# Prompt's pair sums, expert choice and softmax differences moved from the prompt's top-k stage into the latents' recurrence

## What is computed

```python
# for the prompt (phase 0), then for the latents (phase 1)
h = rmsnorm(x) * (1 + scale) + shift
q, k, v, xr, xg, ga, gr = split(h @ w_in)
xc = dwconv(xr)                              # width 4
r, ig = sigmoid(blockdiag(xc, w_a)), sigmoid(blockdiag(xc, w_i))    # two directions
a = exp(-8 * r * softplus(-lam)); b = sqrt(1 - a*a) * ig * xc
rnn = scan(a, b)                             # the recurrence, forward and backward
r_out = (rnn * gelu(xg)) @ w_rnn_o
...
x = x + g_a * ((sigmoid(ga) * a_out + sigmoid(gr) * r_out) @ w_out)
# PEER, per token and per head of 8:
s  = h @ w_q @ keys                          # 2 x 128 scores
st, it = top_k(s, 16)                        # for each of the two halves
cand = st[0][:, None] + st[1][None, :]       # the pair sums, 256
best, pos = top_k(cand, 16)
eidx = (it[0] * 128 + it[1])[pos]            # the experts: rows of u_tab and v_tab
g = softmax(best)
y = sum_k g_k * gelu(u_tab[eidx_k] . x) * v_tab[eidx_k]
```

## Time and profile before

| | |
|---|---|
| median of 3 runs | 2406.46 us |
| profiled execution | 2402.87 us, span 2401.0 us |
| DVE busy | 1880.0 us, 78% of the span |
| PE busy | 1722.7 us, 72% |
| chain that ended last | DVE 41%, PE 18%, DMA 17%, POOL 9%, issue 7% |
| prompt's top-k stage on DVE | 252.4 to 321.4 us |
| latents' recurrence on DVE | 321.7 to 494.4 us |

### The profile page before, as it was taken

The page is one execution under the profiler, slowest core; times in us unless marked ns, Lnnn a source line. Parts: engine busy times, 40 slices in busy tenths (PEclk is TensorE's granted clock), DMA queues, the critical chain, the costliest instruction groups (busy, mean ns, idle before and its releaser), DMA issues.

```text
span 2401.0 us, 21809 instructions
## 1 busy us (share of the span) xinstructions
PE 1722.7 (72%) x6720; PEld 1066.3 (44%) x6720; DVE 1880.0 (78%) x3982; ACT 501.9 (21%) x1271; POOL 1038.8 (43%) x1028
## 2 busy tenths in 40 slices
PE   5798879999888998961326666599999995000285
PEld 4788734544365466530113334466566664000131
DVE  3642779756895576899999998888787977999955
ACT  2632226510042001110015565700000000000010
POOL 0000001146433443435756775344344456777574
PEclk8899889999999999985557777899999998555599
DMA  9797824469745875867989999699999999999997
GB/s 343 256 308 261 261 88 140 140 234 370 280 142 200 299 270 198 306 211 288 409 332 346 410 392 345 197 359 411 413 409 412 411 411 411 409 410 410 354 409 302
DMA packets 290092, 753.71 MB, mean 314 GB/s; under 512 B 21801, under 2 KB 133177, under 8 KB 288441
## 3 DMA queue, kind: packets, MB, share of 16 engines
q0 software_dynamic: 147456, 536.94, 58.8%
q1 hardware_dynamic: 142520, 215.39, 25.4%
HBM read 740.93 MB, written 11.31 MB: 313 GB/s over the span
## 4 chain that ended last, share of the span: by engine, by line
DVE 41%; PE 18%; DMA 17%; POOL 9%; issue 7%; ACT 3%; PEld 2%; SPq 1%; DVEq 0%; POOLq 0%; PEldq 0%; ACTq 0%
DMA attn<-in_peer_u_dram,eidx 7%; PE bank L831 6%; DVE big L1602 5%; DVE attn L1602 4%; PE pair L831 4%; DMA ring_more<-in_peer_u_dram,eidx 4%; DVE work L1602 3%; PE bank L1015 3%; POOL work L2194 3%; POOL big L2194 2%; POOL attn L2194 2%; DMA ring_more<-in_peer_v_dram,eidx 2%; DVE ring_more L1602 2%; PE bank L1063 2%; ACT work L1135 2%
## 5 line engine op out<-in xcount | busy, mean ns | idle before, releaser
L1063 PE MATMUL bank<-big,work 128*128 128x512 f32 x176 | 107.0, 745 | 365.5 <-ACT work L1135 263.0
L831 PE MATMUL bank<-big 128*128 128x512 f32 (+1 forms) x1120 | 340.8, 464 | 33.1 <-DVEq L1470 19.8
L2194 POOL DMA_INDIRECT h_all<-in_peer_u_dram,eidx x109 | 122.1, 1120 | 529.0 <-DVEq L2063 322.0
L831 PE MATMUL pair<-big 128*128 128x128 f32 (+1 forms) x1216 | 333.5, 431 | 10.5 <-issue 9.0
L1108 PE MATMUL bank<-h_all,big 128*128 128x512 f32 x608 | 267.9, 597 | 5.3 <-DMA h_all<-in_peer_v_dram 5.3
L831 PEld LDWEIGHTS bank<-big 128*128 128x128 f32 x1120 | 184.0, 202 | 183.7 <-issue 177.4
L831 PEld LDWEIGHTS pair<-big 128*128 128x128 f32 x1216 | 185.8, 195 | 144.2 <-issue 142.0
L2194 POOL DMA_INDIRECT attn<-in_peer_u_dram,eidx x166 | 163.2, 983 | 165.7 <-DVE dots L1602 100.1
L1063 PEld LDWEIGHTS bank<-big,work 128*128 128x128 f32 x176 | 37.2, 229 | 421.9 <-issue 389.7
L1108 PEld LDWEIGHTS bank<-h_all,big 128*128 128x128 f32 x608 | 180.6, 297 | 88.4 <-DMA h_all<-in_peer_v_dram 6.0
L1602 DVE CUSTOM_DVE_ANT_0 attn<-attn,pair 128x1024 f32<-128x1024 f32 x166 | 199.5, 1218 | 22.5 <-DMA attn<-in_peer_u_dram,eidx 20.2
(11 more groups left out here) (319 smaller groups left out, 3100.4 us busy)
## 6 DMA issues: line engine op xcount, KB each, us to landing
big<-in_w_in_dram SPq DMA_DIRECT2D x44, 1024.0 KB, 9.4
h_all<-in_peer_v_dram SPq DMA_DIRECT2D x76, 512.0 KB, 6.8
big<-in_w_ada_dram SPq DMA_DIRECT2D x24, 1024.0 KB, 9.3
big<-in_peer_w_q_dram SPq DMA_DIRECT2D x16, 1024.0 KB, 8.2
gf_row<-in_peer_v_dram SPq DMA_DIRECT2D x26, 512.0 KB, 6.7
work<-in_peer_v_dram SPq DMA_DIRECT2D x26, 512.0 KB, 6.8
big<-in_w_rnn_o_dram SPq DMA_DIRECT2D x8, 1024.0 KB, 6.6
big<-in_w_attn_o_dram SPq DMA_DIRECT2D x8, 1024.0 KB, 7.4
```

The source lines that it names most:

```text
L831: last = nc.tensor.matmul(u[:, 0:n], w[:, k, col:col + P], src[:, k, 0:n], start=(k == 0), stop=(k == KD - 1))
L1063: last = nc.tensor.matmul(psum[i][:, :], diag[:, (n - 1) % DIAGS, :], ring[r][:, i * 512:(i + 1) * 512], start=(k == first_by_tensor[c]), ...
L2194: g.indirect_dma_start(dst, None, ins["peer_" + table][0], bass.IndirectOffsetOnAxis(ap=eidx[:, c, k:k + 1], axis=0)).then_inc(landed, 16)
```

## The change

`best_sums`, `route0` and `best_diffs` leave the prompt's top-k stage. `route0(h)` now runs `best_sums` itself, all eight heads come from `serve` (LEFT0 is 8), and the last one is followed by `best_diffs`. In the recurrence of phase 1 the middle `serve` is `serve(0)` in blocks 0 to 4 and `serve(3)` in blocks 5 to 7. `gelu_dots(0)` stays where it is.

```diff
-            HEADS_IN_LOOP = 3
-            LEFT0 = PH - HEADS_IN_LOOP
+            LEFT0 = PH
 
             def route0(h):
 
+                best_sums(0, h)
                 experts(0, h, h + 1)
                 ids(0, h, h + 1)
+                if h == PH - 1:
+                    best_diffs(0)
...
-                    serve(1)
+                    serve(1 if ph == 0 else 3 if j >= 5 else 0)
                     if j + 1 < LB:
                         gelu_out(j + 1)
...
                         topk(-1, hp, scores0[:, hp, :])
                         if hp + 1 in ada_after:
                             add_bias(ada_after[hp + 1])
-                        if hp % 2:
-                            best_sums(0, hp // 2)
-                            if hp // 2 < HEADS_IN_LOOP:
-                                route0(hp // 2)
-                        if hp == HP - 1:
-                            best_diffs(0)
                         continue
```

## The result

The changed kernel takes 2417.78 us, median of five runs (2417.55 to 2422.06), against 2406.46 us (2403.84 to 2408.01). The medians differ by 11.3 us, where 10.7 was predicted; the ratio over all runs is 1.0053 with a 95% interval of 1.004 to 1.0067, so the change makes the kernel slower by some 10 to 16 us. The work left the top-k stage as intended and PE's wait of 13.21 us disappeared; a later wait took its place.

The account below looks back on a forecast made before the run. PE and DVE run at almost the same pace; with the moved work DVE bounds the recurrence. 8.2 us later bank plus 2.5 us cold clock gives +10.7 us: 2413.6 us profiled, 2417.2 us median, range 2405 to 2423.

Parts of the forecast that it names:

- What leaves the top-k stage, and where DVE starts: Top-k stage to first `serve`: 36.5 us removed, state copy at 289.9, DVE's first route 16.1 us earlier.
- The work ahead of the bank: Recurrence: 29.5 us more DVE work before the bank for `xr` 7 is free, which comes 8.2 us later.
- PE's clock: At `xr` 7: PE restarts at 1.2 GHz after its new wait, costing 2.5 us (bounds 0 to 2.9).
- From `xr` 7 to `ro` 0: Recurrence's end: PE's 62.4 us stay; added rows lie beside them, DVE's slack shrinks to 7 us.
- rival C: Recurrence, merge and flush: more cold clock, late rows and flush cost 16.3 us in all, 2422.8 us; chance 0.10.
- Behind `ro` 0: Merge and later: all shifts as a whole; two rows left to the flush cost 0, or 2.3 us uncovered.
- Rival A: Recurrence: moved work fits in DVE's idle time, kernel 16.1 us faster, 2390.3 us; chance 0.10.
- Rival B: At `xr` 0's weights or the DMA-bound 541 to 602 us: shift absorbed, 2406.5 to 2411.3 us; chance 0.13.

Follow-up runs that it names:

- e10_after_again: The changed kernel once more, no edit, on the same chip as e9: 2420.96 us against 2408.41 for the kernel before, ratio 1.0055.
- e1: Changed kernel with the eight `best_sums` and `best_diffs` back in the top-k stage: 2402.42 us against 2407.88 for the kernel before, ratio 0.9978.
- e5: As e4, but the middle `serve` gives three rows in blocks 6 and 7 only: 2392.93 us against 2407.03 for the kernel before, ratio 0.994.
- e7: As e4, with the middle `serve` behind `gelu_out(j + 1)`: 2395.28 us against 2407.03 for the kernel before, ratio 0.9944.
- e9: Changed kernel with nine unread matmuls in PE's wait between `v` 0 and `xr` 7: 2415.60 us against 2408.41 for the kernel before, ratio 1.003.
- e2: Changed kernel with the middle `serve` behind `gelu_out(j + 1)` in every block: 2415.28 us against 2407.88 for the kernel before, ratio 1.0027.
- e8: Changed kernel with five rows in place of three in the middle of blocks 6 and 7: 2418.39 us against 2407.03 before, ratio 1.0041.
- e4: Changed kernel with three heads back in the top-k stage, five and `best_diffs` served in the recurrence: 2399.72 us against 2407.88 before, ratio 0.9966.
- e6: Changed kernel with seven unread matmuls in PE's wait between `v` 0 and `xr` 7: 2415.73 us against 2407.03 for the kernel before, ratio 1.0039.

## Why the prediction was right

- *What leaves the top-k stage, and where DVE starts.* The state copy was put at 289.9 and stands at 291.37, with 1.8 us of offset, which `xr` 0 has too. The first `serve` starts 17.7 us behind `xr` 0 (311.72 - 294.01); 17.4 were predicted.
- *The work ahead of the bank.* A delay of 8.2 us was worked out (451.7 less 443.57 is 8.1). `xr` 7 comes 8.9 us later, counted from `xr` 0, and 8.4 us later in e10_after_again. The difference is made of small things, among them 1.99 us of wait at `conv(1)` in place of 1.7, and handovers of 0.2 us at each of the three added heads. e1 to e5 and e7 moved this work in both directions and by single rows, and the bank followed each time to within 1.5 us of what was expected (of the middle, where a range was given).
- *PE's clock.* 2.5 us were taken; 16.35 against 13.97 us is 2.4, at a granted clock of 0.50 in the first 4.6 us. In e9, where the wait is filled, they are gone.
- *From `xr` 7 to `ro` 0.* Nothing else changed: 69.55 us to DVE's first output whenever PE didn't restart cold, in four kernels and in e9. DVE's slack shrank from 10.89 to 5.17 us; I had said 7. But 10.89 less the 4.6 us of the four added rows is 6.3, and the six rows behind the recurrence took 8.9 us in place of 7.75, since two of them waited 0.28 and 1.36 us for their gathers; that leaves 5.2, and is the start of rival C.
- *Behind `ro` 0.* In this execution the merge and the rotary steps took 2.2 us longer (`ro` 0 to the first scores of attention: 669.53 - 519.25 = 150.3 against 148.1 us). In e10, the same kernel, they took 0.5 us longer. Over all twelve profiled executions here they took 147.3 to 150.4 us, and e2, e7 and e8 lie above the kernel before while e4, e5 and e6 lie below it. So I take the 2.2 us for scatter and not for a price of the change. The chance given to C was for this. The two rows that fall to the flush were covered, as the sum had it: DVE's wait ahead of the second merge's first output shrank from 13.03 to 10.38 us. The remaining 4 us between the two profiled executions lie behind attention. The profiled execution is one of two of the five that took 4.3 us more than the median, and where they come from stays open.
- *Rival A* fails at the point where it was said to be decided: 29.5 us were moved, and 21.4 could be taken. e4 and e5 are the other side of that point. They keep some of this work out of the recurrence (three heads) and bring 8 to 14 us. The idea of interleaving was sound; the amount and the place of it were not.
- *Rival B*: nothing was absorbed. PE's wait for the weights of `xr` 0 is 5.85 us in place of 5.89, and counted from `xr` 0 the first scores of attention come 13.4 us later than before, 11.0 us in e10.
- *How close the number is.* The steps up to `ro` 0 add up to 11.3 us in one trace and 10.5 in the other, and 10.7 was worked out: that is the mechanism. That the first median agrees to 0.6 us is luck in part: three of its five runs took 2417.6 to 2417.8 us and two 2422.1, and the second comparison gives 12.6 us.

What I had not seen beforehand: DVE's dead time between the top-k stage and `xr` 0, 11.97 + 4.34 us, which my own numbers held, is the place in which the sums cost nothing. I used it only to say that the gain was limited.

## What to carry to other kernels

Before moving work out of a stage, look where its engine would stand still afterwards, and leave there as much as fills that time: here 16 us of the 36 moved became idle time. In the stage that receives it, find the one handover on which the other engine waits next (here the rotary step of `k` 0), and add up the work ahead of it; 4.6 us of work added behind it (e8) cost 1 us on the first output, and work ahead of it cost its full time. Two engines that run at nearly the same pace (16.5 and 17.2 us a block) hid nothing from each other here.

## What the runs showed of the hardware

Ahead of `xr` 7 a wait of 2.71 us on PE cost 1.7 us in e6, while waits of 2.38 us, 3.42 us (e4) and 1.00 us (e9) cost nothing, and those of 5.2 to 8.7 us cost 2.0 to 3.0 us. In e6 the granted clock was 1.00 through the wait and fell to 0.50 only about 1 us into the work behind it. So the fall can come late, when the engine is already at work.

Whether a short wait costs anything isn't told by its length. The wait ahead of `gates(3)` shows it best, since it is nearly the same in both executions of the changed kernel. Timeline of PE in the changed kernel, then in e10_after_again:

```profile
379.26 3.70 PE L849 MATMUL pair<-work,big 128*128 128x512 f32 x8 [3.66 <-DVEq L1840]
...
380.08 5.40 PE L849 MATMUL pair<-work,big 128*128 128x512 f32 x8 [3.64 <-DVEq L1840]
```

After 3.66 us the eight instructions ran at a granted clock of 1.00 throughout; after 3.64 us the granted clock was 0.70 over the first 2.7 us of work, and they took 1.7 us more. In e8 a wait of 1.98 us ahead of `gates(5)` cost 1.7 us too (5.40 us, granted clock 0.52 over the first 2.7 us), and in e10 one of 2.08 us at the same place cost nothing. None of these reached the end, because PE waited for DVE again behind them. So a short wait of some 2 to 4 us is best given a range in a sum, from nothing to about 2 us.

Why one such wait costs something and the next doesn't stays open. The Trainium skill, TensorE: Matmul & The Clock Gate, section "What's actually happening", says that the window in which the chip looks at PE's activity runs freely and isn't reset when a kernel starts, so that the moment of a change of clock varies. A late fall, and two outcomes of one and the same wait, fit that; no run here was made to test it.
